# One expert group's places by token tiles, its first step inside the routing, and one shared product as a job

## What is computed

```python
h2 = rmsnorm(x, g_ffn).reshape(T, D)                 # 512 x 1024
scores = sigmoid(h2 @ w_router)                      # 512 x 64; top 8 of 64, by groups of 8
idx, wts = route(h2, w_router, router_bias)
# per expert e: y = (silu(h2[tok] @ w_gate[e]) * (h2[tok] @ w_up[e])) @ w_down[e]; acc[tok] += wt * y
moe = routed_experts(h2, idx, wts, w_exp_gate, w_exp_up, w_exp_down) \
    + swiglu(h2, w_sh_gate, w_sh_up, w_sh_down)      # the shared expert, 256 wide
x = x + moe
x = x + sigmoid(rmsnorm(x, g_ple) @ w_ple_gate) * rmsnorm(p @ w_ple_proj, g_ple_post)
```

## Time and profile before

| | |
|---|---|
| median of 3 executions | 984.09 us (983.39 to 986.25) |
| profiled execution | 984.45 us |
| its span in the profile | 982.6 us |
| TensorE matmul busy | 931.6 us, 95% |
| VectorE, ScalarE, GpSimd busy | 360.2, 162.6, 229.7 us |
| mean granted TensorE clock | 0.99 |
| DMA moved | 298.95 MB, mean 304 GB/s |

### The profile page before, as it was taken

How to read it: one execution, slowest core, us unless ns; L and a number is a source line. 1 busy time by engine, 2 the same in 40 slices (tenths; PEclk the granted TensorE clock), 3 DMA queues, 4 the chain that set the end, 5 groups by cost and what they waited for, 6 DMA issues and landing times.

```text
span 982.6 us, 15583 instructions
## 1 busy us (share of the span) xinstructions
PE 931.6 (95%) x6327; PEld 477.7 (49%) x6327; DVE 360.2 (37%) x773; ACT 162.6 (17%) x304; POOL 229.7 (23%) x345
## 2 busy tenths in 40 slices
PE   6999999999999999999999999999969899897798
PEld 4678788888655533333333333333323333332345
DVE  5565673336436743333332111111101111111687
ACT  2001325210011211111111111111111112121021
POOL 4115923162110212222222222211111111101110
PEclk9999999999999999999999999999989999999899
DMA  9940005421493569999999999999999999999972
GB/s 331 333 129 1 1 1 177 167 86 48 135 406 129 214 259 393 399 413 397 409 419 407 411 417 408 404 424 412 390 423 422 421 420 421 417 403 381 374 280 86
DMA packets 81817, 298.95 MB, mean 304 GB/s; under 512 B 9252, under 2 KB 33864, under 8 KB 57553
## 3 DMA queue, kind: packets, MB, share of 16 engines
q1 hardware_dynamic: 68048, 261.09, 67.5%
q0 software_dynamic: 11920, 33.63, 8.7%
q10 hardware_dynamic: 1776, 3.21, 0.9%
HBM read 277.16 MB, written 29.36 MB: 312 GB/s over the span
## 4 chain that ended last, share of the span: by engine, by line
PE 74%; DMA 19%; SPq 3%; DVE 2%; issue 1%; ACT 1%; POOL 0%; ACTq 0%
PE ps L2193 22%; DMA ring<-in_w_exp_up 16%; PE ps L1804 12%; PE ps L2222 9%; PE ps L1954 6%; PE ps L1933 5%; PE ps L2337 4%; PE ps L1760 3%; PE ps L1737 2%; DMA ring<-in_w_exp_down 2%; PE ps L2017 1%; PE ps L2009 1%; PE ps L1766 1%; DMA ring<-accumulator 1%; SPq L463 1%; PE ps L2202 1%
## 5 line engine op out<-in xcount | busy, mean ns | idle before, releaser
L2193 PE MATMUL ps<-ring,gates 128*32 128x512 f32 x2560 | 286.0, 599 | 26.1 <-DMA ring<-in_w_exp_up 25.4
L2193 PEld LDWEIGHTS ps<-ring,gates 128*32 128x32 f32 x2560 | 87.5, 111 | 216.9 <-issue 216.0
L2222 PE MATMUL ps<-ring,poolbuf 128*32 128x512 f32 x1280 | 147.3, 601 | 3.0 <-DMA ring<-in_w_exp_down 2.1
L1551 DVE COPY poolbuf<-ps 128x256 f32<-128x256 f32 x40 | 17.0, 424 | 353.7 <-PE ps L2202 353.7
L2222 PEld LDWEIGHTS ps<-ring,poolbuf 128*32 128x32 f32 x1280 | 38.3, 110 | 85.0 <-issue 83.4
L968 ACT ACTIVATE actT<-ps,qT 128x1024 f32<-128x1024 f32 x40 | 44.5, 1113 | 143.9 <-PE ps L2222 143.9
L781 POOL COPY stage<-qT 128x1 uint32<-128x1 uint32 x40 | 7.2, 180 | 259.3 <-PE ps L1737 231.9
L960 ACT ACTIVATE poolbuf<-ps 128x256 f32<-128x256 f32 x40 | 15.4, 384 | 276.7 <-PE ps L2193 276.7
L1804 PE MATMUL ps<-xrow,ring 128*128 128x256 f32 x256 | 57.9, 381 | 0.1
L1954 PE MATMUL ps<-ring,gates 128*128 128x512 f32 x128 | 56.4, 594 | 0.0
L1737 PE MATMUL ps<-cst,rows 128*128 128x128 f32 x352 | 48.4, 284 | 7.6 <-DVE rows L1064 7.6
(11 more groups left out here) (288 smaller groups left out, 1069.8 us busy)
## 6 DMA issues: line engine op xcount, KB each, us to landing
ring<-in_w_exp_down SPq DMA_DIRECT2D x64, 1024.0 KB, 17.1
ring<-in_w_exp_gate SPq DMA_DIRECT2D x62, 1024.0 KB, 14.1
ring<-in_w_exp_up SPq DMA_DIRECT2D x62, 1024.0 KB, 16.4
ring<-accumulator SPq DMA_DIRECT2D x12, 1024.0 KB, 13.3
ring<-in_w_gate SPq DMA_DIRECT2D x8, 1024.0 KB, 11.6
ring<-in_w_in SPq DMA_DIRECT2D x5, 1024.0 KB, 12.8
xrow<-in_x SPq DMA_DIRECT2D x8, 512.0 KB, 5.1
accumulator<-ring SPq DMA_DIRECT2D x1, 4096.0 KB, 19.9
```

The source lines that it names most:

```text
L2193: last = mm(bank(2 + k)[part, :], hgT[k][:, q, part], pair_view(EXPERT_SLOT[js[c]])[:, q], start=(q == 0), stop=(q == KD - 1))
L2222: last = mm(bank(6 + half)[part, :], eactT[r % 2][:, q, part], w[:, q, half * 512:(half + 1) * 512], start=(q == 0), stop=(q == 1))
```

## The change

Group 0 gets places by token tile. Experts 0 and 1 (`EARLY` = 2) have, in the first 128 places (step 0), 64 each, which only tokens of tiles 0 to 2 may take; their remaining 32 places each stand in step 1 and are for tile 3 alone, so a token of tile 3 is ranked for them by its own tile (with 64 added by the matmul with `halfT`). Experts 2 and 3 have 96 places each over all tiles. Step 1 thus holds strips of experts 0, 1, 2, 2 and step 2 of experts 2, 3, 3, 3. If tiles 0 to 2 give expert 0 or 1 more than 64 tokens, or tile 3 more than 32, the maximum count is set to 512, which starts the further rounds.

Step 0's list and gather then need tiles 0 to 2 only. The last tile's store signals `last_moved` in place of `act_moved`. The list of step 0 is made before `router(3, 0)`, the gather of step 0 is the first after GpSimd's last root, and TensorE's program of the three first steps is written out: up(0) in four pieces between the parts of the sort, up(1), up(2), then down(0) and down(1) after `acts_T(0)` and `lists(1)`. Tile 1's shared product becomes a job (`LATE` = (1, 2, 3), three jobs more; jobs 0 to 10 in steps 24 to 29). Tile 0's last two matmuls stand after up(1). Group 1's loads: `in` of experts 0 and 1 after step 1, of 2 and 3 after step 2, both `down` after down(1). The shared down weights are loaded after the first sort matmul.

```diff
-LATE = (2, 3)
+LATE = (1, 2, 3)
-JOB_STEP = [SMALL_AT + n // 2 for n in range(8)] + [SMALL_AT + 6 + n // 2 for n in range(4 * NT)]
+N_LATE = 3 * len(LATE)
+JOB_DOWN, JOB_PLE = N_LATE + 2, N_LATE + 2 + 2 * NT
+JOB_STEP = [SMALL_AT + n // 2 for n in range(JOB_DOWN)] + [SMALL_AT + 6 + n // 2 for n in range(4 * NT)]
+EARLY, EARLY_CAP = 2, 64
+FIRST_STRIPS = [[0, 0, 1, 1], [0, 1, 2, 2], [2, 3, 3, 3]]
...
-SH_BANK = [7, 3, 5, 5]
+SH_BANK = [7, 5, 5, 5]
+SH_ORDER = [4, 5, 6, 7, 0, 1, 2, 3]
...
-            sp.wait_ge(act_moved, 16 + 16 * NT)
+            sp.wait_ge(act_moved, 16 * NT)
+            sp.wait_ge(last_moved, 16)
             for j in range(2):
                 sp.dma_start(w_ple[j], t["w_ple_proj"][0][j * P:(j + 1) * P, :]).then_inc(late_loaded, 16)
+            sp.wait_ge(sorted_ps, 1)
+            sp.dma_start(w_shd, t["w_sh_down"][0].rearrange("(j p) n -> p j n", p=P)).then_inc(late_loaded, 16)
             sp.wait_ge(order_ready, 1)
-
-            sp.wait_ge(tokw_ready, 1)
-            sp.dma_start(w_shd, t["w_sh_down"][0].rearrange("(j p) n -> p j n", p=P)).then_inc(late_loaded, 16)
...
+                if g == 1:
+                    in_used(1)
+                    load_in(pos, e[0])
+                    load_in(pos + 1, e[1])
+                    in_used(2)
+                    load_in(pos + 2, e[2])
+                    load_in(pos + 3, e[3])
+                    down_used(1)
+                    load_down(pos, e[0])
+                    load_down(pos + 1, e[1])
+                    return e[2:]
...
-                pool.wait_ge(rows_listed, STEP_OF[r][0] + 1)
+                pool.wait_ge(rows_listed, STEP_OF[r][0] + 2 if r else 1)
+                if r == 1:
+                    pool.wait_ge(last_moved, 16)
...
-            pool.wait_ge(act_moved, 16 + 16 * NT)
+            pool.wait_ge(act_moved, 16 * NT)
...
-                act.dma_start(h2_rows[i], rows[:, i, :]).then_inc(act_moved, 16)
+                act.dma_start(h2_rows[i], rows[:, i, :]).then_inc(act_moved if i < NT - 1 else last_moved, 16)
...
-            shared_silu_of(0)
-            act.wait_ge(hgT_ps, 1)
...
+            rows_lo(0, 0)
             rows_hi(0, 0)
-            shared_silu_of(1)
+            act.wait_ge(maskedT_ps, 1)
+            nc.scalar.activation(rankT, bank(6)[0:NE, :], ACT.Copy).then_inc(maskedT_ready, 1)
+            nc.scalar.activation(scT, bank(3)[0:NE, :], ACT.Copy).then_inc(maskedT_ready, 1)
+            rows_lo(1, 1)
+            rows_hi(1, 1)
...
-            places(0, rank3[:, :, 0:FIXED], ((0, 3),))
+            first_places((0, LAST), (0, EARLY), 1, EARLY_CAP, 0)
+            first_places((0, LAST), (EARLY, GROUP), 1, CAP, EARLY * CAP)
             residual(3, 1)
...
+            dve.wait_ge(list_ps, 1)
+            rows_of(0, 1, early_found[:, 0:1, :])
+            second_T(3, 1)
             gained_rows(3, 0)
-            second_T(3, 1)
             gained_rows(3, 1)
             select(3)
             weights_masked(0, 3)
             ranks(3, 4)
-            places(0, rank3[:, :, 0:FIXED], ((3, 4),))
+            first_places((LAST, NT), (0, EARLY), EARLY_CAP + 1, REST_CAP, REST)
+            first_places((LAST, NT), (EARLY, GROUP), 1, CAP, EARLY * CAP)
...
+            link(nc.vector.tensor_tensor(over, bank(4)[0:1, EARLY_AT:EARLY_AT + 2 * EARLY],
+                                         cst[0:1, C_LIMIT:C_LIMIT + 2 * EARLY], ALU.is_gt))
...
-            dve.wait_ge(shared_ps, 2)
...
-            shared_mult(1)
...
+                for e in range(2, experts):
+                    link(nc.vector.tensor_tensor(slot_wr[:, r, :], slot_wr[:, r, :], mine[:, :, e, :], ALU.add))
...
+                if r == 0:
+                    shared_mult(0)
+                    shift_late((0, LAST), EARLY_CAP, REST_CAP)
+                    shift_late((LAST, NT), CAP, LAST * P + REST_CAP - CAP)
...
+                if e0:
+                    mm(at[:, 0:e0], oneT[:, :], halfT[:, :], start=True, stop=False)
+                    mm(at[:, 0:e0], triT[:, :], selb[:, i * NE:i * NE + e0], start=False, stop=True)
...
-            def up(r):
+            def up(r, q0=0, q1=KD):
...
-                if r == 1:
-                    pe.wait_ge(shared_act, 2)
+                if r == 2:
+                    pe.wait_ge(eact_ready, 1)
...
+            pe.wait_ge(place_ready, 3)
+            list_rows(0, early_list(0), 0, NT - 1).then_inc(list_ps, 1)
+            router(3, 0)
...
             rows_T(0)
-            shared_up(1, 4, 8)
-            for r in range(STEPS):
+            pe.wait_ge(place_ready, 6)
+            for s in range(1, steps_of(0)):
+                last = list_rows(0, early_list(s), s)
+            last.then_inc(list_ps, 1)
...
+            up(0, 0, 1)
...
+            up(0, 1, 3)
...
+            up(0, 3, 5)
+            rows_T(1)
+            up(0, 5, 8)
+            up(1, 0, 6)
+            rows_T(2)
+            up(1, 6, 8)
+            shared_up(0, 6, 8)
+            up(2)
+            acts_T(0)
+            lists(1)
+            down(0)
+            acts_T(1)
+            down(1)
+            rows_T(3)
+            lists(2)
+            for r in range(steps_of(0), STEPS):
```

More of the change, by code:

```diff
@@ L71 @@
 C_PAIR2 = C_PAIR + 6
-C_IC = C_PAIR2 + 4
+C_FIRST = C_PAIR2 + 4
+C_LIMIT = C_FIRST + len(FIRST_STRIPS) * GROUP
+C_IC = C_LIMIT + 2 * EARLY
 C_ALL = C_IC + NG * PAD
 def jobs_of(step, slot):
-    return [n for n, at in enumerate(JOB_STEP) if at == step and n % 2 == slot]
+    return [n for n, at in enumerate(JOB_STEP) if at == step][slot:slot + 1]
 def cap_of(g):
@@ L282, in build @@
         zero_row = ring[:, 10, 0:D]
+        first_wsum, first_own = (rest[:, k * 24:(k + 1) * 24].rearrange("p (s e c) -> p s e c", e=GROUP, c=2)
+                                 for k in range(2))
         pair_sum, pair_own = (small[:, 40 + k * 12:52 + k * 12].rearrange("p (s e c) -> p s e c", e=2, c=2)
@@ L2055, in _ @@
             out_proj(3, 1, 6, 8)
-            router(3, 0)
-            second_T(3, 1)
-            pe.wait_ge(pT_ready, 2)
-            shared_up(0, 0, 1)
-            router(3, 1)
-            shared_up(0, 1, 6)
-            rank(3)
-            for q in range(NT):
-                mm(bank(4)[0:NE, 256:256 + NE], oneT[:, 0:NE], selb[:, q * NE:(q + 1) * NE], start=(q == 0),
-                   stop=(q == NT - 1))
-            for q in range(NT):
-                last = mm(bank(4)[0:NE, 256 + NE:257 + NE], selb[:, q * NE:(q + 1) * NE], oneT[:, 0:1],
-                          start=(q == 0), stop=(q == NT - 1))
@@ L2187, in up @@
                     experts_loaded()
-                for q in range(KD):
+                for q in range(q0, q1):
                     if r == STEPS - 1 and q == KD // 2:
@@ new lines, in _ @@
+            second_T(3, 1)
+            pe.wait_ge(pT_ready, 2)
+            shared_up(0, 0, 1)
+            router(3, 1)
+            shared_up(0, 1, 6)
+            rank(3)
+            for q in range(NT):
+                mm(bank(4)[0:NE, 256:256 + NE], oneT[:, 0:NE], selb[:, q * NE:(q + 1) * NE], start=(q == 0),
+                   stop=(q == NT - 1))
+            for q in range(NT):
+                last = mm(bank(4)[0:NE, 256 + NE:257 + NE], selb[:, q * NE:(q + 1) * NE], oneT[:, 0:1],
+                          start=(q == 0), stop=(q == NT - 1))
@@ new lines, in _ @@
+            for e, tiles in ((0, range(NT - 1)), (EARLY, range(NT - 1, NT))):
+                for q in tiles:
+                    last = mm(bank(4)[0:1, EARLY_AT + e:EARLY_AT + e + EARLY], oneT[:, 0:1],
+                              selb[:, q * NE:q * NE + EARLY], start=(q == tiles[0]), stop=(q == tiles[-1]))
+            last.then_inc(rank_ps, 1)
+            rows_T(0)
+            pe.wait_ge(place_ready, 6)
+            for s in range(1, steps_of(0)):
+                last = list_rows(0, early_list(s), s)
@@ new lines, in _ @@
+            last.then_inc(list_ps, 1)
+            pe.wait_ge(masked_ready, 2)
+            for i in range(NT):
+                nc.tensor.transpose(bank(6)[0:NE, i * P:(i + 1) * P], r_rank[:, i * NE:(i + 1) * NE], ident)
+                last = nc.tensor.transpose(bank(3)[0:NE, i * P:(i + 1) * P], r_w[:, i * NE:(i + 1) * NE], ident)
+            last.then_inc(maskedT_ps, 1)
+            up(0, 0, 1)
+            pe.wait_ge(perm_ready, 1)
+            mm(bank(5)[0:1, 336:336 + NE], cst[0:NE, C_P:C_P + 1], perm, start=True, stop=True)
@@ new lines, in _ @@
+            mm(bank(5)[0:1, 336 + NE:336 + 2 * NE], cnt_col, perm, start=True, stop=True).then_inc(sorted_ps, 1)
+            up(0, 1, 3)
+            pe.wait_ge(maskedT_ready, 2)
+            for i in range(NT):
+                mm(bank(6)[:, i * NE:(i + 1) * NE], rankT[:, i * P:(i + 1) * P], perm, start=True, stop=True)
+                last = mm(bank(6)[:, NR + i * NE:NR + (i + 1) * NE], scT[:, i * P:(i + 1) * P], perm,
+                          start=True, stop=True)
+            last.then_inc(sorted_ps, 1)
@@ L2252, in _ @@
                     job(n)
```

(3 more changed lines are left out.)

205 lines of the change are left out of this document (116 added, 89 removed).

## The result

| | before | changed |
|---|---|---|
| median of 12 executions | 985.47 us | 987.94 us |
| lowest and highest | 983.39, 986.25 | 985.81, 992.48 |
| ratio, 95% interval | | 1.0032 [1.0022, 1.0042] |
| span of the profiled execution | 982.6 us | 985.5 us |
| step 3's up product starts (timeline) | 376.53 us | 379.87 us |

The changed kernel is slower by 0.3%, some 3.2 us by the ratio (the medians differ by 2.5), where 4.1 less was forecast. All times of the kernel before are now of more executions than the three of the prediction; each ratio is to the executions that were timed with the kernel in question. (The chain of waits gives the mark before as 376.71; here the timeline's 376.53 is used throughout.)

The account below looks back on a forecast made before the run. TensorE was taken to pace the expert stage's first half, weight loads its second. Terms −7.26 −0.8 +0.5 +1.6 +1.5 +0.4 gave −4.1 us at step 3, handed on to 980.0 us against the 984.09 median; range 977.0 to 983.8.

Parts of the forecast that it names:

- What bounds the kernel in its first half: Expert stage: TensorE paces its first half with DMA just as full, so an earlier step 3 is handed on.
- The wait before down(1): Before step 1's down product: TensorE waits 1.5 us because VectorE is still working off three lists.
- The second gather: In the routing: goes out near 334.0, lands by 339.3, wanted at 339.9, so nothing is lost.
- The job: Tile 1's shared product in the small groups: cost 0, hidden under a 6.69 us wait before up(30).
- the first gather: Before the last tile's routing: lands after 6.1 us, at 331.25, so TensorE waits 1.6 us.
- rival B: First gather takes 8.7 us, TensorE waits 4.2, a slower clock adds 1.7; 984.3 us, chance 0.12.
- Step 3's gather: Goes out at 362.75, wanted at 370.4; in time at 6.9 us, 1.0 late at 8.7; 0.4 us taken.
- Small work: Early list, small matmuls in the last rank and counts, one more place operation: +0.5 us.
- The loads gain more than TensorE: Group 1's loads start near 351.2 and end 5.5 us earlier, so TensorE's 4.1 us is handed on.
- rival C: The change does not reach the end, since DMA is full from 376 on; 984.1 us, chance 0.10.
- A: Rival: gathers land in time, served beside the loads, and both gather terms vanish; 978.0 us, chance 0.15.
- D: Rival: slower, the late product in step 28 delays step 31's loads, at most 7.9 us; 987.9 us, chance 0.07.

Follow-up runs that it names:

- e1: The changed kernel with four useless 512-column products before the first transposes of gathered rows; ratio 0.9999 to the kernel before.
- e3: The changed kernel with group 1's lists before the third up product and VectorE's list work before its step 0 copy; ratio 1.0012 to the kernel before.
- e4: The kernel before with only tile 1's shared product taken out of the routing and made a late job; ratio 1.0009 to the kernel before.
- e5: The kernel before with only group 1's loads issued in the changed kernel's order; ratio 1.0030 to the kernel before.
- e9: The kernel before with four useless products put right before step 3's up product; ratio 1.0049 to the kernel before.
- e6: The changed kernel with the sort ahead of the first rows' transposes and all of step 0's up product; ratio 1.0042 to the kernel before.
- e7: The changed kernel with the 512 KB PLE gain row loaded behind the last tile's store and PLE weights; ratio 1.0002 to the kernel before.
- e2: The changed kernel with tile 0's last two shared products moved before the first transposes of gathered rows; ratio 1.0003 to the kernel before.
- e11: The kernel of e8 but with the sort left between the pieces of step 0's up product; ratio 0.9976 to the kernel before.
- e10: The kernel of e8 plus the 512 KB PLE gain row loaded behind the last store; 980.70 us, ratio 0.9955 to the kernel before.
- e8: The changed kernel with e2, e3 and e6 together and step 3's row transposes before down(1); 981.72 us, ratio 0.9956 to the kernel before.

## Why the prediction was wrong

**What held.** What bounds the kernel in its first half: a late step 3 is handed on. In the profiled executions of the change, e1, e3, e4, e5 and e9 the shift at the mark is found again at step 17 within 0.05 us. (In e6 the second fall makes it 5.45; in e7, profiled in its slowest execution, it grows from 0.4 to 2.3 with waits for up weights, two of them 0.75 and 0.34.) In all the runs with a late mark the ratio agrees with that shift within its interval. The wait before down(1): 1.67 us for 1.5 forecast, though moving the lists did not remove it but changed what is waited for (e3). The second gather: in time. The job: cost 0 was right in size, and partly by luck. I had the loads for step 31 landed by 748.9, before TensorE wants them; in e4 TensorE waited for them until 751.51 (in the change until 753.95), and the clock that no longer falls before up(30) gave back what this cost.

**The term that failed: the first gather.** I took 6.1 us for its landing, between two rows, and 1.6 us of wait; it took 7.7 and 3.55. That is +1.95 (1.6 from the landing, the rest from a start 0.25 later and a want 0.1 earlier than worked out). The store of the same moment, which I had held for proof of a quick landing, itself took 6.9 instead of 5.9 with the gather beside it. e7 shows what it hangs on: bytes in flight.

**The term that was missing from the sum: the clock.** I had a fall of the clock only in rival B, at 1.7 us and a chance of 0.12, priced from one late product that ran at 8.77 for 7.07 us. It cost 2.7 us (e1), for it covered transposes, the sort and the first piece of up(0), all of them on the path. I had also taken the 2.43 us of idle in that row for the least that brings a fall (it is so in e2's expectation). In these runs 1.60 (e2) and 1.81 (e7) did not, but 1.80 did in e5, 2.19 after 0.34 in e6, and there 1.43 after 1.67 too. At step 25 a wait of 2.24 us left the clock alone in the change and one of 2.25 us in e4 did not (up product 7.07 and 8.77). So the length of the wait alone does not tell, a wait of 1.6 us, as I forecast it, already stood at the edge, and a fall belonged in the forecast's own range.

**Step 3's gather**, 1.48 us of wait for 0.4: with all of group 1's gate and up loads sent out in two bunches it took 9.3 us, beyond the 8.7 that I had as the upper end. e5 isolates this: 11.2 us.

**Small work.** −4.1 with +1.95, +2.7, +1.1 and +0.2 makes +1.85; the mark has +3.2 against the chain's 376.71. The missing 1.3 us stand in the timelines of e1 and of the kernel before, both at full clock, counted from each group's start to the next instruction or its own end: the up products of steps 0 to 2 take 21.45 us for 21.01, the four row transposes 4.16 for 3.81, the two down products 7.22 for 6.92 and the two `acts_T` 0.85 for 0.68. Sixteen half matmuls of a piece take 1.85 us where a quarter of a whole product takes 1.75. I had costed cutting and reordering the products at nothing. No run isolates it.

**The loads.** "The loads gain more than TensorE" rested on the first four going out at 351.2; they went at 357.2. It was also only half right as a rule. By the ratios, gains at the mark arrive in part: −4.1 gives −2.4 us (e11), −6.2 gives −4.4 (e10), −1.4 gives nothing that can be told (e2); −5.3 gives −4.3 (e8), but there the interval reaches −5.6. The traces show where a head start goes, which is rival C in a weak form: DMA is full from 360 on, and TensorE comes to wait for loads. e8's shift is −5.3 up to step 11, −4.7 at step 17 and −3.3 at step 18, before whose up product stands a wait of 1.65 us for its weights; e10 and e11 go from −6.1 and −4.1 at step 4 to −3.9 and −1.9 at step 18, with waits of 1.80 and 1.75 there. Behind step 18 the shifts swing by one to two microseconds, by waits and by falls of the clock that differ between executions (step 25: 8.77 us in the profiled execution of the kernel before, 7.07 in the change), so how much of the rest is lost for good stays open; a mark moved early with the loads' issue held would be needed.

**The rivals.** B had the mechanism (a slow gather, then the clock) with too small a price for the clock, and none for step 3's gather or the small work, and gave 984.3; A was refuted by the 7.7 us, and with it the estimate of 3.2 us from the Trainium skill ("DMA: Bandwidth & Descriptors", on the anatomy of one DMA by the GpSimd path) for this place: here a 512 KB gather took 3.5 us with DMA nearly idle (66 GB/s) and 6.0 to 11.2 with loads in flight. D's number, 987.9, is what was measured, 987.94, but that is an accident: e4 shows its wait before step 31, and of its price of 7.9 us nothing at the end that can be told.

**The mended version** beats both kernels: e8 at 0.9956 [0.9943, 0.9969]. So the idea of the change, step 0 inside the routing, gains the 4 us forecast once the gap at its first gather is filled and the lists stand where VectorE is free. What moving the lists would give the kernel before without the rest of the change was not run.

## What to carry to other kernels

A wait on TensorE is priced with the clock that may fall behind it: the 3.55 us here cost another 2.7, and 3.7 us of useless products in their place made the kernel faster. A gather moved earlier must be priced with the bytes in flight at its new place, from the slowest row that resembles it; a bunch of loads sent ahead of a gather can delay it by microseconds (11.2 us for 6.9 in e5). What is hidden under a long idle wait late in the kernel (the job, 6.9 us under 6.69) can be nearly free, and the place to look for such room is the waits' rows, not the busy share; the loads that it holds up must be followed one step further. And a mark read from one profiled execution is compared with that execution's own span before it is held against a median.

## What the runs showed of the hardware

- The granted clock fell to 0.50, 1.2 GHz, after idle times of TensorE as short as 1.80 us (e5), and after 1.67 and 1.43 us some 5 us apart (e6), but not after 1.81 (e7) or 2.24 (the change, step 25). The same pair of waits in the same order of work, 1.67 and 1.48, left it alone in the change. After 3.55 us it was down for some 7 us.
- A gather of 512 KB landed after 3.5 us while DMA moved 66 GB/s, after 4.6 at 123 GB/s (the change's second), after 6.0 and 7.7 at 336 and 322, and after 6.9, 9.3 and 11.2 at 407, 414 and 394. With DMA full the rate no longer tells how long it takes.
- Taking 7.26 us of matmuls out of TensorE's path (e4) left the time as it was or slightly longer: 4.1 us became waits, and some 3.4 went into the slower clock behind them (transposes 1.97 for 1.05 us, the first up product 9.52 for 7.07).
